# Building the S5 input matrix ahead of x, and finishing each block of tokens of a residual by itself

## The reference

```python
step = exp(log_step); lr = minimum(lam_re, -1e-4); li = lam_im
mag = exp(lr * step)
ar = mag * cos(li * step); ai = mag * sin(li * step)
inv = 1.0 / (lr * lr + li * li)
fr = ((ar - 1.0) * lr + ai * li) * inv
fi = (ai * lr - (ar - 1.0) * li) * inv
bbr = fr[..., None] * br - fi[..., None] * bi      # the input matrix
bbi = fr[..., None] * bi + fi[..., None] * br
bu = einsum(u, bbr), einsum(u, bbi)                # 32 groups, 64 complex states each
x_t = (ar + i ai) * x_(t-1) + bu_t                 # along the 256 tokens
```

```python
x = x + g_m * _rmsnorm(y, norm_g[layer, 1])        # per token: sum of squares, root, reciprocal
```

## Time and profile before

| | |
|---|---|
| median of three executions | 1636.27 us |
| the profiled execution | 1638.53 us, its span 1636.8 us |
| TensorE busy | 1541.8 us, 94% of the span |
| VectorE, ScalarE, GpSimd busy | 408.2, 219.4, 95.8 us (25%, 13%, 6%) |
| the chain that ended last | TensorE 81%, DMA 6%, issue 2%, VectorE 1% |
| mean DMA rate | 298 GB/s; 410 to 417 GB/s in most of the second half |
| mean granted clock of TensorE | 0.986 |

### The profile page before, as it was taken

The page is one execution under the profiler, slowest core; times in us unless marked ns, Lnnn a source line. Parts: engine busy times, 40 slices in busy tenths (PEclk is TensorE's granted clock), DMA queues, the critical chain, the costliest instruction groups (busy, mean ns, idle before and its releaser), DMA issues.

```text
span 1636.8 us, 23980 instructions
## 1 busy us (share of the span) xinstructions
PE 1541.8 (94%) x10657; PEld 898.7 (55%) x10658; DVE 408.2 (25%) x851; ACT 219.4 (13%) x428; POOL 95.8 (6%) x106
## 2 busy tenths in 40 slices
PE   8899999999999999989999998999899989998986
PEld 6676587777588855554333353456666653433322
DVE  6695212232245556121000001020010020100102
ACT  3422200000321144220000000000000000000001
POOL 7153000000000012000000000000000000000000
PEclk9999999999999999988999999999999999999999
DMA  9577476664563425368999986999999959999995
GB/s 342 181 257 266 164 265 255 230 228 158 193 248 120 157 96 194 138 240 311 413 415 413 348 291 257 417 417 411 412 406 405 393 213 410 415 415 412 415 417 238
DMA packets 160084, 490.01 MB, mean 299 GB/s; under 512 B 15888, under 2 KB 18896, under 8 KB 147664
## 3 DMA queue, kind: packets, MB, share of 16 engines
q1 hardware_dynamic: 153024, 482.52, 76.3%
q10 hardware_dynamic: 6928, 5.56, 1.1%
HBM read 486.97 MB, written 1.08 MB: 298 GB/s over the span
## 4 chain that ended last, share of the span: by engine, by line
PE 81%; DMA 6%; issue 2%; DVE 1%; ACT 0%; SPq 0%; DVEq 0%
PE bank L1796 28%; PE bank L1324 20%; PE bank L1832 13%; PE bank L1532 5%; DMA ring<-in_moe_w_down 5%; PE bank L1641 3%; PE bank L1706 3%; PE bank L1768 2%; DMA arena<-in_moe_w_gate 1%; PE bank L1813 1%; PE bank L1656 1%; PE bank L1349 0%; PE bank L1373 0%; PE bank L1338 0%; PE bank L1522 0%
## 5 line engine op out<-in xcount | busy, mean ns | idle before, releaser
L1796 PE MATMUL bank<-ring,arena 128*32 128x256 f32 (+3 forms) x3376 | 351.5, 427 | 32.2 <-issue 26.2
L1324 PE MATMUL bank<-arena,ring 128*128 128x256 f32 x1264 | 280.9, 381 | 1.4 <-ACT arena L688 1.1
L1796 PEld LDWEIGHTS bank<-ring,arena 128*32 128x32 f32 (+1 forms) x3376 | 159.2, 120 | 215.6 <-issue 168.4
L1324 PEld LDWEIGHTS bank<-arena,ring 128*128 128x128 f32 x1264 | 238.8, 191 | 34.1 <-ACT arena L688 1.5
L1832 PE MATMUL bank<-ring,arena 128*32 128x256 f32 (+1 forms) x1568 | 191.4, 463 | 11.5 <-DMA ring<-in_moe_w_down 10.1
L1243 DVE TENSOR_TENSOR arena<-arena,bank 128x512 f32<-128x512 f32 (+2 forms) x44 | 24.4, 577 | 644.1 <-PE bank L1796 644.1
L1796 PE MATMUL bank<-arena 128*32 128x256 f32 (+3 forms) x1488 | 159.5, 424 | 8.6 <-issue 5.0
L1832 PEld LDWEIGHTS bank<-ring,arena 128*32 128x32 f32 (+1 forms) x1568 | 75.9, 120 | 117.9 <-issue 79.8
L1796 PEld LDWEIGHTS bank<-arena 128*32 128x32 f32 (+1 forms) x1488 | 75.6, 121 | 85.7 <-issue 55.9
L827 ACT ACTIVATE arena<-bank 128x512 f32<-128x512 f32 (+2 forms) x44 | 21.1, 508 | 637.8 <-PE bank L1813 535.0
L1532 PE MATMUL bank<-ring,arena 128*128 128x512 f32 x176 | 76.7, 594 | 1.5 <-PE bank L1324 1.5
(11 more groups left out here) (280 smaller groups left out, 1173.3 us busy)
## 6 DMA issues: line engine op xcount, KB each, us to landing
ring<-in_moe_w_down SPq DMA_DIRECT2D x86, 1024.0 KB, 16.5
ring<-in_moe_w_gate SPq DMA_DIRECT2D x82, 1024.0 KB, 17.1
ring<-in_moe_w_up SPq DMA_DIRECT2D x70, 1024.0 KB, 18.0
ring<-in_ada_w SPq DMA_DIRECT2D x24, 2048.0 KB, 9.7
arena<-in_moe_w_up SPq DMA_DIRECT2D x42, 1024.0 KB, 17.1
arena<-in_moe_w_gate SPq DMA_DIRECT2D x30, 1024.0 KB, 19.1
arena<-in_moe_w_down SPq DMA_DIRECT2D x26, 1024.0 KB, 16.0
ring<-in_m_w_in SPq DMA_DIRECT2D x12, 2048.0 KB, 8.9
```

Source lines behind the costliest of these rows:

```text
L1324: ins = mm(out_, l, r, start=i == 0, stop=i == len(pairs) - 1, **kw)
L1796: ins = mm(ps[base + b // per][m * h:m * h + m, w * (b % per):w * (b % per) + w], hcur3[:, kc, m * b:m * b + m], sl[:, kc - half * rows, w ...
```

## The change

1. VectorE makes the 15 parameter instructions, `bb` and `bx` directly behind the angles; only quarter 0 of the turnings stays ahead of the scaled x, and quarters 1, 2 and 3 follow it.
2. ScalarE takes the two small sines behind its first modulation copy; it copies the first four turned pairs between the third and the fourth modulation copy, and the last four behind `ct`.
3. TensorE turns the first four pairs (now through banks 4 and 5) between `ada_turn(2)` and `ada_mm(3)`, with no warm-up products behind the third piece, and the last four behind `s5_in(1)`. The four chains of the input projection follow each other.
4. In `residual` the sum, root, reciprocal and update are made for each block of tokens by itself; block 0 is finished between the third and the fourth bank. ScalarE takes two roots of one column.

```diff
@@ -614,8 +614,11 @@
                     act.wait_ge(s["out_mm"], 4 * (n - 1) + k + 1)
                     c.inc(f(junk_sq[:, i], ps[base + i][:, :], ACT.Square,
                             scale=scale, accum_out=stat[:, 4 + i:5 + i]), "sq_done")
-                act.wait_ge(s["root_in"], n)
-                c.inc(f(stat[:, 10:12], stat[:, 8:10], ACT.Sqrt, bias=eps[:, 0:1], scale=1.0 / D), "root_done")
+                    if k >= 2:
+                        b = k - 2
+                        act.wait_ge(s["root_in"], 2 * (n - 1) + b + 1)
+                        c.inc(f(stat[:, 10 + b:11 + b], stat[:, 8 + b:9 + b], ACT.Sqrt, bias=eps[:, 0:1], scale=1.0 / D),
+                              "root_done")

@@ -643,12 +646,20 @@
                 c.inc(f(prm[rows_h, STEP], log_step[rows_h, h:2 * NQ:2], ACT.Exp), "step_exp")
             act.wait_ge(s["step_ready"], 1)
             c.inc(f(prm[:, MAG], prm[:, LRSTEP], ACT.Exp), "mag_ready")
-            for i in range(4):
-                ada(i)
-            hT_high(1, 1, mod[:, 0, 0])
+            ada(0)
             act.wait_ge(s["turn_ready"], 1)
             for row in (SIN1, PB):
                 c.inc(f(prm[:, row], prm[:, row], ACT.Sin, scale=TWO_PI), "turn_sin")
+
+            def bt_copy(i):
+                act.wait_ge(s["b_turned"], i + 1)
+                c.inc(f(bt[:, 2 * i:2 * i + 2], bank((4 if i < 4 else 6) + i % 2, 2, 2, P), ACT.Copy), "bt_ready")
+            ada(1)
+            ada(2)
+            for i in range(4):
+                bt_copy(i)
+            ada(3)
+            hT_high(1, 1, mod[:, 0, 0])
 
             def table_sines(half):
                 act.wait_ge(s["tab_ready"], half + 1)
@@ -656,9 +667,6 @@
                 for k in range(2):
                     c.inc(f(tables[:, k, qs], tables[:, k, qs], ACT.Sin, scale=TWO_PI), "tab_sin")
             table_sines(0)
-            for i in range(8):
-                act.wait_ge(s["b_turned"], i + 1)
-                c.inc(f(bt[:, 2 * i:2 * i + 2], bank(6 + i % 2, 2, 2, P), ACT.Copy), "bt_ready")
             act.wait_ge(s["band_ready"], 6)
             for h in range(2):
                 act.wait_ge(s["u_mm"], h + 1)
@@ -672,6 +680,8 @@
                         src = bank(i, 4, P)[64 * h:64 * h + 64, :, at:at + 16]
                         dst = ct[64 * h:64 * h + 64, j:NQ:4, i, at:at + 16]
                         c.inc(f(dst, src, ACT.Copy), "ct_ready")
+            for i in range(4, 8):
+                bt_copy(i)
             table_sines(1)
 
             def pool_to_sbuf(i):
@@ -912,24 +922,30 @@
 
             def residual(n, n_sq, n_root, rows_, base=0, prescaled=False):
 
+                def finish(b):
+
+                    col = slice(2 + b, 3 + b)
+                    root(n_root + b)
+                    c.then(v.reciprocal(rst[:, col], stat[:, 10 + b:11 + b]), step)
+                    if prescaled:
+                        c.then(tt(rst[:, col], rst[:, col], rst[:, 4 + b:5 + b], ALU.mult), step)
+                    dve.wait_ge(s[step], c.n[step])
+                    c.inc(stt(x[:, b], tmp[:, b], rst[:, col], x[:, b], ALU.mult, ALU.add), "x_ready")
                 dve.wait_ge(s["grow_ready"], 2 * n)
                 for k, i in enumerate(OUT_ORDER[n - 1]):
                     dve.wait_ge(s["sq_done"], n_sq - 3 + k)
-                    if k == 3:
-                        c.inc(tt(stat[:, 8:10], stat[:, 4:8:2], stat[:, 5:8:2], ALU.add), "root_in")
+                    if i % 2:
+                        b = i // 2
+                        c.inc(tt(stat[:, 8 + b:9 + b], stat[:, 4 + 2 * b:5 + 2 * b], stat[:, 5 + 2 * b:6 + 2 * b], ALU.add),
+                              "root_in")
                     at = slice(HALF * (i % 2), HALF * (i % 2) + HALF)
                     c.inc(tt(tmp[:, i // 2, at], ps[base + i][:, :], rows_[:, at], ALU.mult), step)
-                n_tmp = c.n[step]
-                root(n_root)
-                c.then(v.reciprocal(rst[:, 2:4], stat[:, 10:12]), step)
-                if prescaled:
-                    c.then(tt(rst[:, 2:4], rst[:, 2:4], rst[:, 4:6], ALU.mult), step)
-                dve.wait_ge(s[step], n_tmp)
-                for b in range(NB):
-                    c.inc(stt(x[:, b], tmp[:, b], rst[:, 2 + b:3 + b], x[:, b], ALU.mult, ALU.add), "x_ready")
-                    if n == 3 and b == 0:
-                        dve.wait_ge(s["bias_mm"], 1)
-                        c.inc(tt(r_bias, r_bias, ps[0][:, 0:NE], ALU.add), "bias_taken")
+                    if k == 2:
+                        finish(0)
+                finish(1)
+                if n == 3:
+                    dve.wait_ge(s["bias_mm"], 1)
+                    c.inc(tt(r_bias, r_bias, ps[0][:, 0:NE], ALU.add), "bias_taken")
                 dve.wait_ge(s["x_ready"], 2 * n)
 
 
@@ -953,21 +969,6 @@
             c.inc(v.tensor_copy(prm[:, SIN1], prm[:, TAU]), step)
             c.then(ts(prm[:, PB], prm[:, TAU], 0.25, None, ALU.is_gt), step)
             c.inc(stt(prm[:, PB], prm[:, TAU], 0.25, prm[:, PB], ALU.add, ALU.subtract), "turn_ready")
-
-            def table_turns(quarter):
-                qs = slice(quarter * NQ // 4, (quarter + 1) * NQ // 4)
-                tS, tC = tables[:, 0, qs], tables[:, 1, qs]
-                c.then(tt(tS, t_row.unsqueeze(1).broadcast_to([P, NQ // 4, TOK]),
-                          prm[:, TAU, qs].unsqueeze(2).broadcast_to([P, NQ // 4, TOK]), ALU.mult), step)
-                c.then(ts(tC, tS, ROUND, -ROUND, ALU.add, ALU.add), step)
-                c.then(tt(tS, tS, tC, ALU.subtract), step)
-                c.then(ts(tC, tS, 0.25, None, ALU.is_gt), step)
-                c.inc(stt(tC, tS, 0.25, tC, ALU.add, ALU.subtract), "tab_ready" if quarter % 2 else step)
-            table_turns(0)
-            table_turns(1)
-            mods(0, 4)
-            scale_cols(1, 1, mod[:, 0, 1], norm_col(0, 0))
-            hT_low(1, mod[:, 0, 0])
 
             dve.wait_ge(s["turn_sin"], 2)
             dve.wait_ge(s["mag_ready"], 1)
@@ -997,6 +998,21 @@
                     c.inc(v.tensor_copy(bx[64 * h:64 * h + 64, :, j:NQ:4, at:at + 16],
                                         bb[64 * h:64 * h + 64, :, j:NQ:4, :]), "bx_ready")
 
+            def table_turns(quarter):
+                qs = slice(quarter * NQ // 4, (quarter + 1) * NQ // 4)
+                tS, tC = tables[:, 0, qs], tables[:, 1, qs]
+                c.then(tt(tS, t_row.unsqueeze(1).broadcast_to([P, NQ // 4, TOK]),
+                          prm[:, TAU, qs].unsqueeze(2).broadcast_to([P, NQ // 4, TOK]), ALU.mult), step)
+                c.then(ts(tC, tS, ROUND, -ROUND, ALU.add, ALU.add), step)
+                c.then(tt(tS, tS, tC, ALU.subtract), step)
+                c.then(ts(tC, tS, 0.25, None, ALU.is_gt), step)
+                c.inc(stt(tC, tS, 0.25, tC, ALU.add, ALU.subtract), "tab_ready" if quarter % 2 else step)
+            table_turns(0)
+            mods(0, 4)
+            scale_cols(1, 1, mod[:, 0, 1], norm_col(0, 0))
+            hT_low(1, mod[:, 0, 0])
+
+            table_turns(1)
             table_turns(2)
             table_turns(3)
 
@@ -1053,7 +1069,7 @@
             dve.wait_ge(s["tile_used"], AT["ada1", 9] + 1)
             mods(NADA, 2 * NADA - 2)
             gate_cols(3, mod[:, 1, 2], norm_col(1, 1))
-            residual(2, 12, 2, grow)
+            residual(2, 12, 3, grow)
 
 
             norm_x(3)
@@ -1154,10 +1170,10 @@
                 for n in (2 * m, 2 * m + 1):
                     c.inc(ts(yT1[:, n], bank(m % 4, 2, TOK)[:, n % 2], cols[:, 1, C_M2G + n:C_M2G + n + 1], None, ALU.mult),
                           "yT1_a")
-            root(3)
+            root(5)
             c.inc(v.reciprocal(rst[:, 4:6], stat[:, 14:16]), "rg_ready")
             dve.wait_ge(s["rg_ready"], 1)
-            residual(3, 20, 4, grow1, 4, True)
+            residual(3, 20, 6, grow1, 4, True)
 
 
             gate_cols(4, mod[:, 1, 5], norm_col(1, 3))
@@ -1384,31 +1400,37 @@
             stay_warm(WARM_C, 5)
             pe.wait_ge(s["c_ready"], 1)
             pe.wait_ge(s["consts"], 9)
+            def b_turn(i):
+
+                if i == 0:
+                    pe.wait_ge(s["bx_ready"], 8)
+                if i == 4:
+                    pe.wait_ge(s["mod_ready"], 1)
+                if i >= 2:
+                    pe.wait_ge(s["bt_ready"], i - 1)
+                for k in range(4):
+                    ins = turn(ps[(4 if i < 4 else 6) + i % 2][:, P * k:P * k + P], bx[:, k % 2, 2 * i + k // 2], ident[:, :])
+                ins.then_inc(s["b_turned"], 1)
             for i in range(3):
                 ada_mm(i)
                 ada_turn(i)
-                stay_warm(WARM_ADA, 5)
+                if i < 2:
+                    stay_warm(WARM_ADA, 5)
+            for i in range(4):
+                b_turn(i)
             ada_mm(3)
             pe.wait_ge(s["cols_ready"], 1)
             turn_x(1)
             ada_turn(3)
 
             w = slot(arrived(AT["mixin", 1]), KC, HALF)
```

(17 more changed lines are left out.)

## The result

The changed kernel took 1627.88 us (median of six executions, 1626.38 to 1631.0) against 1636.38 for the kernel before (six, 1635.2 to 1638.62): ratio 0.9945, interval 0.9934 to 0.9957. By the ratio that is 9.0 us less (7.0 to 10.8 by its interval; the two medians differ by 8.5). The profiled execution took 1628.11, its span is 1626.4, 10.4 us less than before.

A forecast was written before the change was run, and what follows sets the result against it. TensorE was taken to bound the kernel (81% of the span). 3.97 us gained in the front, less 1.7 for the clock, plus 0 for the residuals, made 2.3: 1634.0 us against 1636.27, range 1630.0 to 1637.0.

The forecast's parts named there:

- When `bx` is ready: Front, VectorE: bx, the matrix of the S5 inputs, would be ready at 33.4 us, instead of 48.51.
- the walk: Front: VectorE's instructions followed one by one, each held until GpSimd's running instruction ends; it gave bx at 33.4 us.
- the bound 28.3: Front: when bx would be ready if GpSimd did not disturb VectorE, after B's imaginary part lands at 24.2 us.
- TensorE to the mark: Front: 27.5 us from the first turn of bx to the long pool input product, reached at 61.0 instead of 64.97.
- The clock: Front, TensorE: half clock for 3.4 us over the four turns and following multiplication, costing 1.7 us, bounds 0 to 2.3.
- What else is moved: Front: VectorE's first quarter of turnings ends at 38.6 us, before it is wanted at 40.4, so costs nothing.
- The residuals: The three residuals: finishing block 0 early gains 0, with 0.4 us either way.
- I therefore make the sum at this one mark, 64.97, and carry the difference unchanged to the end: From the long pool input product to the kernel's end: the front's gain, 2.3 us after the clock's cost, passes unchanged.
- Rival 1: Front: the clock holds or bx comes earlier, 4.0 to 6.7 us gained, time 1629.6 to 1632.3; chance 0.40.
- Rival 2: To the end: the saving is hidden, for instance by the expert weights' stream, time 1636.3 us; chance 0.09.
- rival 3: Front: GpSimd holds bx back to 38.1 us, time up to 1639.3 us; chance 0.06.
- S: Front: start of TensorE's first four turns, forecast 33.5; gain becomes loss at 37.5 with full clock, 35.8 with 1.7 lost.

The follow-up runs named there:

- e7: The changed kernel with GpSimd making window bands 2 to 4 only once bx is ready; 1628.2 us, ratio 0.9931.
- e3: The changed kernel with 11 more warm-up products at tile 1 of the dense SwiGLU; 1634.44 us, ratio 0.9982.
- e1: The kernel before with all of the change except its residual part and ScalarE's roots; 1628.1 us, ratio 0.9939.
- e9: The changed kernel with 6 more warm-up products in a wait of the routing, which moves the experts' code later; 1635.94 us, ratio 0.9967.
- e2: The kernel before with only the residual part of the change; 1638.04 us, ratio 0.9999.
- e14: The kernel before with 3 warm-up products (12 instructions) fewer in a wait ahead of the experts; 1630.94 us, ratio 0.9963.
- e5: The kernel before with 6 of 10 warm-up products left out of an early TensorE wait; 1632.73 us, ratio 0.9969.
- e10: The changed kernel with 6 more warm-up products in the routing and as many instructions fewer at the start; 1630.43 us, ratio 0.9931.
- e11: The changed kernel with window bands 2 to 4 after bx, 6 warm-up products in each of two routing waits, a shorter start; 1627.89 us, ratio 0.9911.

## Why the prediction failed, point by point

- **When `bx` is ready: right.** Forecast 33.4 by the walk, measured 32.72 (31.42 and 1.30). The blocking it rests on is in the trace after, 1.38 against 0.43, and e7 removes it: 28.28 against the bound 28.3. The Trainium skill, SBUF — State Buffer, section Who interferes with whom, agrees with both. Of the 0.7 us, 0.56 is GpSimd's earlier end, 30.19 instead of 30.75; the lengths that the walk itself states (0.52, twice 0.64, 1.29, with 0.07 between, twice over, and two more products of 1.29) add up from 20.57 to 30.0, so its 30.75 was not their sum.
- **TensorE to the mark: right.** From the first turn to the mark the forecast was 27.5 plus 1.7 for the clock, 29.2; measured 29.34. The four chains had no idle, as forecast. That the sum is met to 0.1 is luck: the clock cost 0.5 more, and turning c and the two state inputs 0.4 less (0.90 and 1.73 between starts, not 1.03 and 1.99).
- **The clock: right in kind, too small for this trace.** Forecast 1.7, bounds 0 to 2.3, measured 2.2 to 2.3, near the upper bound. It fell at 31.3, in the gap, and not with the turns, and stayed at half for 6.8 us, not 3.4. In other executions of this front the same two steps cost 1.7 (e3) and 1.3 (e1), and in e9 it was 1.3 there and 1.7 more over the first chain, so the term is off by what executions differ in, not in kind. The gain at the mark is 2.86 against 2.3 forecast: bx 0.7 earlier, the clock 0.5 dearer, c and the state inputs 0.4 shorter. The first chain's start at 43.01 is within the 41.5 to 43.2 given.
- **What else is moved: right.** VectorE ended its first quarter at 37.95, before the 40.4 from which it would have cost.
- **The residuals: right.** Nothing, by e2 and by the 2.93 us that stand ahead of and behind the first two. TensorE of after behind the first residual and behind the third, to be read against the earlier trace rows:

```profile
192.43 1.91 PE L1382 MATMUL bank<-ident,arena 128*128 128x128 f32 x16
```

```profile
715.39 1.92 PE L1340 MATMUL bank<-rw,mod 128*128 128x8 f32 x16 [0.41 <-PE bank L1731]
```

  195.36 less 192.43 and 718.32 less 715.39 are both 2.93.
- **"I therefore make the sum at this one mark, 64.97, and carry the difference unchanged to the end": this step failed.** The difference was found again at 192, 442 and 715 us and was 3.07 at the gather. Behind the gather the stage gave another 7.3 in the profiled executions, some 6 in the medians (6.1 by e14's ratio, 5.1 by e5's, 5.5 between the medians of e9 and e10). The step took time as the only thing that passes from the front to the end. The number of instructions passes too. I priced the removed warm-up products by the clock of the front alone and gave no price to the shift of all later code, though the page showed 2% of "issue" on the chain and the chain of before showed two stops with five matmuls between them. The sum with this term is 2.9 + 5.1 or 2.9 + 6.1, 8.0 to 9.0 us, and the measured ratio of 0.9945 is 9.0 (7.0 to 10.8).
- **The rivals.** None held. Rival 1 named the right side for a wrong reason: neither did the clock hold nor did `bx` come at 31.7. Rival 2 (not carried) and rival 3 (GpSimd holds `bx` to 38.1) did not occur; the drift between S and its turning point of 35.8 was 3 us. A rival "the removed instructions move the code of a later stage" was missing, and so the range ended at 1630.0.
- **What stays open.** In e5 and e11 the clock fell once more around expert 1 without a second stop, and the same kernel before took from 1632.74 to 1643.12 us in one session. Which execution loses clock there is not explained by the place. e3's stop of 7.30 us at 1330 goes with code as well, four instruction packets from 1328.56 on where after has three, the last landing 1.6 us ahead of the first matmul at 1337.59; why one more is fetched there is not known. What makes the second packet wait until 3.0 to 3.7 us behind the first is not seen either. How much of the 6 us is the stop itself and how much the lower clock behind it differs from execution to execution, and was read in one pair.

## What to carry to other kernels

An edit that only adds or removes instructions, warm-up products included, moves all later code of that engine; where the chain shows "issue" behind a jump, look for a second stop a few instructions further on, set the packets of the instruction queue beside it, and try the same kernel with a few dummy instructions more or fewer, since this can be worth more than the edit (here 6 us against 3). When an early stage is compared by experiments, keep the instruction count ahead of the later stages constant, or the verdict mixes the two. Read a mark in several executions of the same code before a difference there is believed: here it moved by 1 us and more with nothing changed. Two-input VectorE work in short instructions under long GpSimd instructions should be walked through instruction by instruction; moving GpSimd's work out of the way gave 4 us at the mark, once the operand's DMA had landed.
